# Moving the softmax scaling of twelve attention head pairs from VectorE to GpSimd, in a two-block transformer kernel on one core

## The reference

```
qa, ka, va, qb, kb, vb, qc, kc, vc, g = split(rmsnorm(x) @ w_in)
# 4 "differential" heads (a): two softmaxes over the same values, subtracted
p = softmax(q k^T * scale + bias, causal)          # two maps per head
attn = p[:, :, 0] - lam * p[:, :, 1];  o = attn @ v
# 8 sliding-window heads (b): a sink logit joins each softmax's denominator
# 8 block-attention heads (c): at 256 tokens, plain causal attention in one block
mix = ga*(ya @ w_oa) + gb*(yb @ w_ob) + gc*(yc @ w_oc)
x = x + rmsnorm(mix @ w_out)                       # then an FFN, then a second block
```

## Time and profile before

| | us |
|---|---|
| three runs | 2681.15, 2682.68, 2683.86 |
| median | 2682.68 |
| the profiled execution's own time | 2682.68 |
| its span, first to last instruction | 2680.5 |
| granted TensorE clock, mean of the span | 0.971 |
| PE busy / DVE / ACT / POOL | 2493.0 / 1507.1 / 1249.9 / 189.0 |
| attention of stage A: first score matmul to first gate matmul | 191.25 to 235.90, 44.65 |

### The profile page before, as it was taken

The page is one execution under the profiler, slowest core; times in us unless marked ns, Lnnn a source line. Parts: engine busy times, 40 slices in busy tenths (PEclk is TensorE's granted clock), DMA queues, the critical chain, the costliest instruction groups (busy, mean ns, idle before and its releaser), DMA issues.

```text
span 2680.5 us, 38977 instructions
## 1 busy us (share of the span) xinstructions
PE 2493.0 (93%) x15976; PEld 2072.8 (77%) x15976; DVE 1507.1 (56%) x1964; ACT 1249.9 (47%) x1653; POOL 189.0 (7%) x208
## 2 busy tenths in 40 slices
PE   8999999999999999999999999997999995777877
PEld 6887888887888888878887888786888884677765
DVE  4456454665566666564445444356575543676646
ACT  5446444664555555554444445344354443444333
POOL 2002000000000000000001000000000001343310
PEclk9999999999999999999999999998999996989898
DMA  8756666555655545556555655355466664212062
GB/s 242 238 171 150 210 203 201 202 175 172 213 179 182 178 167 184 181 191 234 198 193 182 193 182 170 114 173 179 165 215 223 216 212 108 48 46 66 15 248 98
DMA packets 242408, 463.41 MB, mean 173 GB/s; under 512 B 9952, under 2 KB 39849, under 8 KB 240480
## 3 DMA queue, kind: packets, MB, share of 16 engines
q1 hardware_dynamic: 223488, 422.08, 47.7%
q0 software_dynamic: 18464, 39.22, 5.3%
q10 hardware_dynamic: 320, 0.13, 0.0%
HBM read 446.66 MB, written 14.74 MB: 172 GB/s over the span
## 4 chain that ended last, share of the span: by engine, by line
PE 44%; DVE 6%; ACT 3%; issue 1%; DMA 1%; POOL 0%; SPq 0%; ACTq 0%; DVEq 0%; POOLq 0%
PE bank L319 12%; PE bank L320 12%; PE bank L321 12%; PE bank L2042 2%; DMA raw<-in_od_w_o 1%; PE bank L1872 1%; PE bank L1894 1%; DVE d_products L2012 1%; PE bank L2130 1%; PE bank L2372 1%; PE bank L2103 0%; DVE d_minus_b L1981 0%; PE bank L1554 0%; DVE d_t L1956 0%; PE bank L1878 0%
## 5 line engine op out<-in xcount | busy, mean ns | idle before, releaser
L256 DVE TENSOR_TENSOR w_low<-raw,w_high 128x1024 fp32r<-128x1024 f32 x768 | 927.1, 1218 | 860.3 <-ACT w_high L250 859.4
L250 ACT ACTIVATE w_high<-raw 128x1024 fp32r<-128x1024 f32 x768 | 805.2, 1057 | 975.7 <-PE bank L321 942.4
L319 PE MATMUL bank<-w_high,b_h_high 128*128 128x512 f32 x704 | 278.3, 395 | 9.0 <-DVE w_low L256 7.5
L321 PE MATMUL bank<-w_high,b_h_low 128*128 128x512 f32 x704 | 275.3, 391 | 0.0
L320 PE MATMUL bank<-w_low,b_h_high 128*128 128x512 f32 x704 | 275.0, 391 | 0.0
L319 PE MATMUL bank<-w_high,a_h_high 128*128 128x512 f32 (+1 forms) x640 | 247.9, 387 | 3.8 <-DVE w_low L256 2.3
L320 PE MATMUL bank<-w_low,a_h_high 128*128 128x512 f32 (+1 forms) x640 | 246.5, 385 | 0.0
L321 PE MATMUL bank<-w_high,a_h_low 128*128 128x512 f32 (+1 forms) x640 | 246.4, 385 | 0.0
L319 PE MATMUL bank<-w_high,d_high 128*128 128x512 f32 x512 | 202.3, 395 | 10.7 <-DVE d_low L2476 10.7
L319 PE MATMUL bank<-w_high,c_x_high 128*128 128x512 f32 x512 | 203.3, 397 | 0.7 <-DVE c_x_low L460 0.7
L320 PE MATMUL bank<-w_low,d_high 128*128 128x512 f32 x512 | 201.4, 393 | 0.0
(11 more groups left out here) (366 smaller groups left out, 3692.1 us busy)
## 6 DMA issues: line engine op xcount, KB each, us to landing
raw<-in_w_up SPq DMA_DIRECT2D x88, 1024.0 KB, 5.0
raw<-in_w_in SPq DMA_DIRECT2D x76, 1024.0 KB, 5.1
raw<-in_ev_w_in SPq DMA_DIRECT2D x48, 1024.0 KB, 5.1
raw<-in_w_down SPq DMA_DIRECT2D x44, 1024.0 KB, 5.0
raw<-in_w_out SPq DMA_DIRECT2D x16, 1024.0 KB, 5.0
raw<-in_ev_w_out SPq DMA_DIRECT2D x16, 1024.0 KB, 5.0
raw<-in_od_w_r SPq DMA_DIRECT2D x16, 1024.0 KB, 5.0
raw<-in_od_w_k SPq DMA_DIRECT2D x16, 1024.0 KB, 5.0
```

The source lines that it names most:

```text
L250: act.activation(wh[n % 4][:, :, 0:width], raw_half, ACT.Copy).then_inc(sem("w_high_made"), 1)
L256: vec.tensor_tensor(wl[n % 4][:, :, 0:width], raw_half, wh[n % 4][:, :, 0:width].bitcast(F32), ALU.subtract).then_inc(sem("w_low_made"), 1)
L319: pe.matmul(b, xh, wh[n][:, k % 2, 0:width], start=(c == 0 and k == 0), stop=False)
L321: mm = pe.matmul(b, xl, wh[n][:, k % 2, 0:width], start=False, stop=(c == j.chunks - 1 and k == 3))
```

## The change

The scaling moves to POOL: a new function `scale(i)` waits until DVE has inverted the row sums (`sums_inverted`), multiplies the tiles by them in place, and raises `probs_scaled`. For kind a it scales the second map alone, and DVE waits for it before it joins the maps. POOL's bias loads are put between the scalings: one head in each of rounds 0 to 3, two heads in each of rounds 4 to 7, none later. The copies out of PSUM are dealt out anew as well: for kinds b and c DVE copies both maps' transposes (ACT copied the first), and DVE copies the result rows of kind a (ACT did). The semaphores `second_probs_turned` and `y_rows_made` go; `probs_turned` and `y_made` count all pairs.

```diff
+        def scale(i):
+            gp.wait_ge(sem("sums_inverted"), i + 1)
+            for u in (1,) if HP[i].kind == "a" else (0, 1):
+                for t, c, w in TILES:
+                    p = PR[i % 3][u][:, c:c + w]
+                    op = gp.tensor_scalar(p, p, small[:, sums_at(i, u, t)], None, ALU.mult)
+            op.then_inc(sem("probs_scaled"), 1)
         for h in range(8):
             load_bias(h)
-        for h in range(8, 20):
-            load_bias(h)
+        for i in range(NP):
+            if i < 4:
+                load_bias(8 + i)
+            elif i < 8:
+                load_bias(4 + 2 * i)
+                load_bias(5 + 2 * i)
+            scale(i)
...
-        gp.wait_ge(sem("y_made"), 8)
+        gp.wait_ge(sem("y_made"), NP)
...
             else:
-                pe.wait_ge(sem("probs_scaled"), i - 3)
+                pe.wait_ge(sem("probs_scaled"), i + 1)
             if i >= 1:
                 pe.wait_ge(sem("probs_turned"), i)
-            if i >= 5:
-                pe.wait_ge(sem("second_probs_turned"), i - 4)
...
             if i >= 2:
-                pe.wait_ge(sem("y_rows_made" if i < 6 else "y_made"), i - 1 if i < 6 else i - 5)
+                pe.wait_ge(sem("y_made"), i - 1)
...
         for i in range(NP + 3):
-            if 2 <= i < NP + 2:
+            if 2 <= i and i - 2 < NP and HP[i - 2].kind == "a":
                 act.wait_ge(sem("probs_transposed"), i - 1)
...
-            if i >= 3:
+            if i >= 3 and HP[i - 3].kind != "a":
...
-                if HP[n].kind == "a":
-                    act.activation(YR[:, :, 128 * n:128 * n + 128], bank[:, c:c + 256].rearrange("p (t e) -> p t e", t=2),
-                                   ACT.Copy).then_inc(sem("y_rows_made"), 1)
...
-                vec.reciprocal(sums, sums).then_inc(sem("a_vec"), 1)
...
-                for u in (1,) if HP[n].kind == "a" else (0, 1):
-                    for t, c, w in TILES:
-                        p = PR[n % 3][u][:, c:c + w]
-                        op = vec.tensor_scalar(p, p, small[:, sums_at(n, u, t)], None, ALU.mult)
...
                 else:
-                    op.then_inc(sem("probs_scaled"), 1)
+                    vec.reciprocal(sums, sums).then_inc(sem("sums_inverted"), 1)
             if 2 <= i < NP + 2 and HP[i - 2].kind != "a":
                 n = i - 2
                 vec.wait_ge(sem("probs_transposed"), n + 1)
-                if n >= 6:
+                if n >= 2:
                     vec.wait_ge(sem("values"), n - 1)
-                vec.tensor_copy(PT[n % 2][1][:, :], PS[1][:, 0:384]).then_inc(sem("second_probs_turned"), 1)
-            if i >= 3 and HP[i - 3].kind != "a":
+                for u in range(2):
+                    op = vec.tensor_copy(PT[n % 2][u][:, :], PS[u][:, 0:384])
+                op.then_inc(sem("probs_turned"), 1)
+            if i >= 3:
...
+                if b == 0:
+                    vec.wait_ge(sem("values"), n + 1)
+                    vec.tensor_copy(YR[:, :, 128 * n:128 * n + 128], bank[:, c:c + 256].rearrange("p (t e) -> p t e", t=2)
+                                    ).then_inc(sem("y_made"), 1)
...
+            if 1 <= i <= NP and HP[i - 1].kind == "a":
+                n = i - 1
+                vec.wait_ge(sem("probs_scaled"), n + 1)
+                for t, c, w in TILES:
+                    p = PR[n % 3][0][:, c:c + w]
+                    op = vec.scalar_tensor_tensor(out=p, in0=p, scalar=small[:, sums_at(n, 0, t)],
+                                                  in1=PR[n % 3][1][:, c:c + w], op0=ALU.mult, op1=ALU.add)
+                op.then_inc(sem("maps_joined"), 1)
```

More of the change, by code:

```diff
@@ L861, in a_act @@
                 act.wait_ge(sem("values"), n + 1)
-                if HP[n].kind == "a":
-                    act.activation(YR[:, :, 128 * n:128 * n + 128], bank[:, c:c + 256].rearrange("p (t e) -> p t e", t=2),
-                                   ACT.Copy).then_inc(sem("y_rows_made"), 1)
-                else:
-                    act.activation(YH[1 if HP[n].kind == "b" else 2][:, n % 4, :], bank[:, c:c + 256], ACT.Copy
-                                   ).then_inc(sem("y_high"), 1)
+                act.activation(YH[1 if HP[n].kind == "b" else 2][:, n % 4, :], bank[:, c:c + 256], ACT.Copy
+                               ).then_inc(sem("y_high"), 1)
             if i == NP:
@@ L976, in a_vec @@
                 sums = small[:, 64 + 4 * n:68 + 4 * n]
-                vec.reciprocal(sums, sums).then_inc(sem("a_vec"), 1)
-                nv += 1
-                vec.wait_ge(sem("a_vec"), nv)
                 if HP[n].kind == "a":
-                    vec.tensor_scalar(small[:, 66 + 4 * n:68 + 4 * n], small[:, 66 + 4 * n:68 + 4 * n], small[:, 37:38],
-                                      None, ALU.mult).then_inc(sem("a_vec"), 1)
+                    vec.reciprocal(sums, sums).then_inc(sem("a_vec"), 1)
                     nv += 1
                     vec.wait_ge(sem("a_vec"), nv)
-                for u in (1,) if HP[n].kind == "a" else (0, 1):
-                    for t, c, w in TILES:
-                        p = PR[n % 3][u][:, c:c + w]
-                        op = vec.tensor_scalar(p, p, small[:, sums_at(n, u, t)], None, ALU.mult)
[L989 to L997, removed]
+                    vec.tensor_scalar(small[:, 66 + 4 * n:68 + 4 * n], small[:, 66 + 4 * n:68 + 4 * n], small[:, 37:38],
+                                      None, ALU.mult).then_inc(sem("sums_inverted"), 1)
                 else:
-                    op.then_inc(sem("probs_scaled"), 1)
+                    vec.reciprocal(sums, sums).then_inc(sem("sums_inverted"), 1)
             if 2 <= i < NP + 2 and HP[i - 2].kind != "a":
@@ L1009, in a_vec @@
                 b = "abc".index(HP[n].kind)
-                vec.wait_ge(sem("y_high"), n - 3)
-                vec.tensor_tensor(YL[b][:, n % 4, :], bank[:, c:c + 256], YH[b][:, n % 4, :].bitcast(F32), ALU.subtract
-                                  ).then_inc(sem("y_made"), 1)
+                if b == 0:
+                    vec.wait_ge(sem("values"), n + 1)
+                    vec.tensor_copy(YR[:, :, 128 * n:128 * n + 128], bank[:, c:c + 256].rearrange("p (t e) -> p t e", t=2)
+                                    ).then_inc(sem("y_made"), 1)
+                else:
+                    vec.wait_ge(sem("y_high"), n - 3)
+                    vec.tensor_tensor(YL[b][:, n % 4, :], bank[:, c:c + 256], YH[b][:, n % 4, :].bitcast(F32), ALU.subtract
+                                      ).then_inc(sem("y_made"), 1)
+            if 1 <= i <= NP and HP[i - 1].kind == "a":
[6 more added lines that the diff above has]
+                op.then_inc(sem("maps_joined"), 1)
         vec.wait_ge(sem("squares_made"), 2)
```

4 lines of the change are left out of this document (1 added, 3 removed).

## The result

The changed kernel takes 2698.61 us (median of four runs, 2694.17 to 2702.56); the kernel before, run beside it, 2681.91 us (2677.12 to 2683.86). The ratio is 1.0064 [1.0043, 1.0086]: slower, by more than the forecast +4.4 us and above the range's end at 2695. The profiled execution took 2698.1 us against 2682.68, +15.4, and its span 2696.1 against 2680.5, +15.6.

What follows compares the result with a forecast made beforehand. PE leads stage A's attention, its 3.37 us round near DVE and ACT's 3.54 ring; POOL's queue would bind in pairs b. +5.1 there less 0.7 in the tail is +4.4 on 2682.68: 2687.1 us, range 2682.5 to 2695.

Steps and rivals of the forecast that it cites:

- 4 A + 5 S - 6.8: Stage A's attention: forecast's added time, 7 S - 6.8 there with kind a at half S; +4.4 us at S 1.60.
- The place and the mechanism: Pairs b: POOL's loads plus scaling, 4.47 us a round against 3.37 to 3.54, delay PE's transposes, +5.1 us; chance 0.56.
- the size of S: POOL's scaling of a b or c pair's two maps: 1.60 us, the middle between copy and tile times small values.
- The upper end of 2.92: Slow end for POOL's two-map scaling, at two full tiles' worst rate, 3.0 ns a column: sum +13.6 us.
- a rival of 0.24: Two-input rate: POOL's scaling takes 1.90, 2.24 or 2.92 us, sum +6.5 to +13.6, 2689 to 2696 us; chance 0.24.
- the prediction's estimate was +2.1: POOL's scaling at the copy's rate, by the skill's statement that one input runs near line rate: sum +2.1 us.
- The granted clock: TensorE in stage A's attention: read as 1.00, the 2.4 GHz level, in the profile before.
- The prediction's tail: Pair 7's transposes to pair 11's sums 10.55 us, gain 0.5; from there to the first gate matmul 4.76, gain 0.2.
- The selection of POOL's routine: Rival: the `ISA` row before POOL's first scaling delays DVE, up to +4.6 us, 2691.7 us; chance 0.08.
- Pairs a: Kind a rounds, DVE waiting for POOL's 0.80 us scaling: 3.25 us instead of 2.96, 0.3 more a round.
- The copies: Kind a's result-row copy on DVE falls in its wait for POOL, free; b and c's second copy adds 0.47 us.
- The ring of 3.54: Pairs b and c: DVE maxima, ACT exponentials and high part, DVE low part, 3.54 us; at most 0.17 a pair winnable.

Runs made afterwards that it cites:

- 58.95 at full clock: Changed kernel plus unread TensorE matmuls before the transposes of pairs 4 to 7, 10 and 11: attention 58.95 us, first score matmul to first gate matmul; whole 2691.61.
- half on DVE: Changed kernel, but in pairs b and c DVE scales map 0 and POOL only map 1: attention 51.25 us; whole kernel 1.0034 to the one before.
- four columns: Changed kernel with each POOL scaling on 4 columns instead of 128 or 256, same waits and order: attention 45.60 us; whole 2685.43.
- fixed factor: Changed kernel with POOL multiplying by 1/128 instead of each row's inverted sum: attention 58.40 us; whole 2696.44.
- two inputs: Changed kernel with POOL's scaling as a product of two tensors, the row values spread along the tile: attention 50.77 us; whole kernel 1.0024 to the one before.

## Why the prediction was wrong, point by point

A is POOL's scaling of one map, as in kind a, and S that of a pair's two maps (of one map in the second row), both as measured.

| variant | A | S | 4 A + 5 S - 6.8 | stretch by it | measured |
|---|---|---|---|---|---|
| changed kernel | 1.47 | 2.93 | +13.7 | 58.4 | 60.37, or 58.95 at full clock |
| half on DVE | 1.46 | 1.46 | +6.3 | 51.0 | 51.25 |
| four columns | 0.52 | 1.06 | +0.6 | 45.2 | 45.60 |
| fixed factor | 1.30 | 2.60 | +11.4 | 56.0 | 58.40, clock 0.91 |
| two inputs | 0.91 | 1.85 | +6.1 | 50.8 | 50.77 |

**The place and the mechanism held.** "From 207.1 on each of four rounds on POOL has two heads' loads, 2.87 us for four DMA issues, and then a scaling of 1.60". The loads measured 2.93 a round. POOL is without a gap, PE waits for it in front of line 770 for pairs 4 to 7, already one pair earlier than the prediction said, and the sum gives four of the five variants within 0.6 us where the clock is 1.00. The fixed factor lies 2.4 above the sum, 1.4 of it a fall of the clock behind pair 7's transposes and most of the rest another in the last pairs.

**The failed step is the size of S.** The prediction says that the multiplication "has one tensor and one value for each row of it, so it lies between the copy and the tile times small values; I take the middle, 0.80 for kind a and 1.60 for b and c". It does not lie between them: 2.45 ns a column is above both, 1.5 times the tile times small values, and lies between the prediction's two rows with two full tensors (2.1 and 3.0). The reasoning counted inputs, and the count of inputs didn't set the time of this operation: with a fixed number in place of the values it is 2.46. Mis-sized, the term cost 4 x 0.67 + 5 x 1.33 = 9.3 us, the larger part of the 11.3 between forecast (+4.4) and stretch (+15.7). The upper end of 2.92, taken from two full tiles at their worst, was right by its value and not by its reason: that is luck, and I gave it a share of a rival of 0.24 instead of the forecast. With it the sum gives 2696, so the range, which ended at 2695, left out the prediction's own upper end.

The Trainium skill, GPSIMD Engine Reference, § Engine selection, puts one input near line rate. By that statement the prediction's estimate was +2.1. The trace agrees for the copy (0.83 ns a column) and disagrees for this product, 2.45.

**The granted clock was not foreseen.** The prediction took 1.00 from before and asked nowhere what PE's new waits would do to it. It fell three times, each time behind a wait for POOL. Two falls were hidden by POOL's rounds; the third, in the last two pairs, cost 1.4 us.

**One wait was left out of the tail.** The prediction's tail gives pair 11's scaling a free POOL. With sums 2.48 us apart (240.29 to 242.77) and a scaling of 2.93 POOL was not free, which cost 0.45. At the forecast's 1.60 it would have been. The three terms, 9.3, 1.4 and 0.45, make 11.2 of the 11.3.

**What held in detail.** The selection of POOL's routine, priced at up to +4.6: in front of the first scaling, DVE's last operation starts at 195.43 and POOL's product at 195.76, no later than in the next pair (199.24 and 199.58), so it cost nothing. POOL had been idle for 1.87 us before, so up to that much may have been hidden. Pairs a: the round is 3.81 us (sums at 199.03 and 202.84) where 3.25 was forecast, 0.73 more from the sums to the join, nearly all of it the scaling, and 0.17 less of join. The copies: the copy of kind a's rows stands in DVE's wait for POOL, which is 1.32 us with it and 1.65 without, as costed; with all scaling on DVE, where there is no such wait, the copies cost 1.0. The tail up to pair 11's sums: 10.57 (232.20 to 242.77), 10.55 forecast. Of the rounds from pair 9 on one is the 3.54 forecast (PE, 240.05 to 243.59); the last is 2.96, POOL's scaling. The ring of 3.54 that bounds what could have been won: confirmed by cutting it.

## What to carry to other kernels

Before work goes to an engine that has a queue of its own to serve, add up that engine's round, every DMA issue in it, and compare it with the round of the others: here 2.93 + 2.93 stood against 3.54, and taking the issues away, or half of the scaling, returned a good half of the loss. Where the operation's form has no row on that engine, measure it by itself first, or forecast from the slow end: the sum was good to about half a microsecond at full clock, and the one guessed rate made it wrong by nine. And a new wait in front of TensorE is to be priced twice, for itself and for the matmuls behind it at the lower clock, though only where nothing slower hides them.

## What the hardware did that I had not expected

- On GpSimd a tensor times one value for each row took 609 ns for 128 and 923 for 256 columns (2.45 ns a column), a tensor times a fixed number 544 and 859, the same product written as tensor times spread tensor 400 and 610 (1.64).
- A DMA issue of this kind took 0.73 us of POOL's time and held up POOL's next operation; on ACT's queue it took 0.37 to 0.90 us beside exponentials that were no longer for it.
- TensorE's granted clock went from 1.00 to 0.50 for some microseconds behind waits of 1 to 2.4 us, and stayed at 1.00 when unread matmuls filled part of them. Behind the same two waits at the end of the attention (1.90 and 0.84 us) it fell in one kernel and not in another.
